# Strassen's scheme for 19 of 22 input slabs of one feed-forward, and a first slab on un-normed x in two others

## The chip, the cores and the metric

The program runs on one NeuronCore of a Trainium2 chip, in one launch. Its time is the device time of that core in microseconds. All engines of the core (TensorE, VectorE, ScalarE, GpSimd, SyncE) are programmed by hand, each with its own instruction stream, and meet through semaphores.

## The reference

Two small decoder blocks stand one after the other on x of 512 tokens by 1024 channels, everything in float32. The first block has two layers with adaptive norm (a hybrid mixer, then a retention mixer), the second has two layers (a MoBA and differential-attention mixer, then a dilated and latent-attention mixer). Each layer ends in a feed-forward of width 2816. The four feed-forwards are what the change is about:

```python
def swiglu(h, w_in, w_out):                      # first block: s0, s1
    g, u = split(h @ w_in)                       # 1024 x 5632
    return (silu(g) * u) @ w_out                 # 2816 x 1024

def conv_ffn(h, w_in, conv_w, conv_b, w_out):    # second block: c0, c1
    u, g = split(h @ w_in)
    g = causal_depthwise_conv(g, conv_w, width=3) + conv_b
    return (gelu(g) * u) @ w_out
```

Their input h is an RMS norm of x over the channels (in the first block with a scale and a shift from the condition).

## The kernel before

x lies transposed in SBUF: channels on the partitions, in eight tiles of 128 x 512 tokens. Every weight matrix comes from HBM in slabs of 1 MB (128 x 2048 float32; 128 x 1408 for the output slabs of the feed-forwards) into three buffers `raw`. To keep float32 precision on TensorE's fast fp32r format, each operand is kept as a high part and a remainder: ScalarE copies `raw` to `whi` (L200, `act_slab`), VectorE subtracts `raw - whi` to `wlo` (L211, `dve_slab`), and each 128x128 block is multiplied three times (`mm3`): hi by hi, lo by hi, hi by lo. There are two buffers each of `whi` and `wlo`, so slab n+2 can be split once slab n is multiplied.

A feed-forward runs in two halves. In a half, eleven input slabs (u = 0 to 10, then 11 to 21) each give one 128 x 512 tile of the gate and one of the other factor: 8 blocks along the channels x 2 tiles x 3 = 48 matmuls of 512 columns, in PSUM banks 2(u mod 2) and the next. In s0 and s1, ScalarE takes the SiLU out of PSUM (L762), VectorE multiplies (L841, the signal `gated`), ScalarE makes the high part (L766) and GpSimd the remainder (L856) of the product. Then eight output slabs multiply these eleven tiles (33 matmuls of 512 columns each), and VectorE adds the result to x. Every engine takes its work in the order in which its program is written; a wait holds all that stands behind it on that engine.

The norm ahead of s0 and s1: the first slab (`pe_first_slab`) is multiplied with x times its gain, not yet divided by the root mean square. Between its third and fourth channel block TensorE sums the squares, ScalarE makes 1/rms (`act_between`, `act_rs`), VectorE (L412), ScalarE (L430, L433) and GpSimd (L440) then write the normed h over the un-normed one behind TensorE, and VectorE multiplies the first slab's two tiles by `rs` (L806). The other 21 slabs take the normed h.

In c0 and c1 all 22 slabs take the un-normed x times gain. The sum of squares stands behind the first slab, and the division by the rms is made in every unit: VectorE takes the gate out of PSUM times `rs` (L820), starts the convolution with one tensor-scalar (L824) and two scalar-tensor-tensor taps (L827, twice), ScalarE takes the GELU (L753), GpSimd multiplies it by `rs` (L853), and VectorE multiplies with the other tile out of PSUM (L841).

## Time and profile before

| | |
|---|---|
| median of three timed runs | 2903.44 us (2899.37 to 2905.34) |
| the profiled execution's own time | 2905.31 us |
| its span in the profile | 2903.5 us |
| mean granted TensorE clock | 0.987 of full speed |
| instructions | 31988 |
| share of the chain that ended last: PE, DVE, ACT, POOL | 88%, 5%, 4%, 1% |
| stretch of s1 (first input slab loaded to the last output slab loaded) | 1250.7 to 1615.7 us |
| stretch of c0, by the same loads | 1883.1 to 2247.2 us |
| DMA, mean over the span | 102 GB/s |

The profile is one execution. PE is TensorE's matmuls, PEld its weight loads, DVE VectorE, ACT ScalarE, POOL GpSimd, SP SyncE. Matmuls are pipelined, so that the records of consecutive ones overlap: what a matmul costs in a stream is the distance between two starts, not its own duration. The chain that ended last goes back from the last instruction to what released each one; "issue" in it is time without a visible cause.

### The profile page before, as it was taken

To read this page: it belongs to the slowest core of one execution; us is meant where nothing else is said; L and a number is where in the kernel's file an instruction comes from. 1 tells how busy PE (TensorE), PEld (TensorE's weight loads), DVE (VectorE), ACT (ScalarE), POOL (GpSimd) and SP (SyncE) were. 2 spreads that over 40 slices of the span, in tenths; PEclk is the share of its full clock that TensorE was granted. 3 is DMA by queue.
4 is the path that set the end of the run, shared out by engine and by line. 5 is a ranking of instruction groups with operands and counts; after the bars stand their busy time and mean duration, and the time that the engine had idled before them with its cause. 6 is when DMAs were issued, how large, how long until landed. Compare 5 with 4: busy or idle time off the path is not lost.

```text
span 2903.5 us, 31988 instructions
## 1 busy us (share of the span) xinstructions
PE 2788.8 (96%) x13306; PEld 2209.4 (76%) x13306; DVE 1409.0 (49%) x2062; ACT 961.3 (33%) x1264; POOL 532.7 (18%) x414
## 2 busy tenths in 40 slices
PE   7998989999999999999999999899999998999998
...
GB/s 241 124 94 85 56 8 145 174 171 227 137 103 98 91 78 85 76 87 103 170 116 75 115 88 74 51 99 78 107 102 79 110 62 62 73 97 75 113 84 69
DMA packets 51088, 296.28 MB, mean 102 GB/s; under 512 B 6617, under 2 KB 6745, under 8 KB 25088
## 3 DMA queue, kind: packets, MB, share of 16 engines
...
## 4 chain that ended last, share of the span: by engine, by line
PE 88%; DVE 5%; ACT 4%; issue 1%; POOL 1%; DMA 0%; SPq 0%; DVEq 0%
PE ps L218 88%; DVE wlo L211 1%; PE ps L1321 1%; ACT whi L200 1%; DMA F<-in_ada 0%; ACT F L1338 0%; DVE F L412 0%; DVE F L2264 0%; DVE hl L416 0%; DVE ada L460 0%; ACT L253 0%; ACT E L2837 0%; DVE F L827 0%; ACT E L2835 0%; ACT hh L430 0%
## 5 line engine op out<-in xcount | busy, mean ns | idle before, releaser
L218 PE MATMUL ps<-hh,whi 128*128 128x512 f32 x2088 | 830.4, 398 | 11.5 <-ACT F L2815 5.8
L218 PE MATMUL ps<-hl,whi 128*128 128x512 f32 x2088 | 816.0, 391 | 0.0
L218 PE MATMUL ps<-hh,wlo 128*128 128x512 f32 x2088 | 815.2, 390 | 0.0
L211 DVE TENSOR_TENSOR wlo<-raw,whi 128x2048 fp32r<-128x2048 f32 (+2 forms) x235 | 496.6, 2113 | 513.7 <-ACT whi L200 511.5
L218 PE MATMUL ps<-R,whi 128*128 128x512 f32 x2080 | 651.4, 392 | 8.0 <-DVE wlo L211 3.1
L200 ACT ACTIVATE whi<-raw 128x2048 fp32r<-128x2048 f32 (+2 forms) x235 | 409.7, 1743 | 748.1 <-PE ps L218 743.6
L218 PEld LDWEIGHTS ps<-hh,whi 128*128 128x128 f32 x2088 | 393.7, 189 | 102.7 <-issue 12.3
L218 PEld LDWEIGHTS ps<-R,whi 128*128 128x128 f32 x2080 | 391.1, 188 | 95.8 <-issue 6.9
L218 PEld LDWEIGHTS ps<-hl,whi 128*128 128x128 f32 x2088 | 393.3, 188 | 83.7
L218 PEld LDWEIGHTS ps<-hh,wlo 128*128 128x128 f32 x2088 | 393.8, 189 | 82.3 <-issue 3.3
L218 PE MATMUL ps<-R,wlo 128*128 128x512 f32 x1040 | 405.4, 390 | 0.0
L218 PEld LDWEIGHTS ps<-R,wlo 128*128 128x128 f32 x1040 | 195.7, 188 | 40.5 <-issue 0.7
L856 POOL TENSOR_TENSOR R<-F,R 128x512 fp32r<-128x512 f32 x88 | 113.8, 1293 | 592.9 <-ACT R L766 592.9
L218 PE MATMUL ps<-F 64*64 64x32 f32 (+11 forms) x1160 | 189.0, 338 | 18.9 <-DMA tmp<-F 2.6
L218 PEld LDWEIGHTS ps<-F 64*64 64x64 f32 (+4 forms) x1160 | 114.8, 164 | 89.8 <-issue 61.9
L853 POOL TENSOR_TENSOR F<-F,rs 128x512 f32<-128x512 f32 x44 | 56.8, 1290 | 453.9 <-ACT F L753 453.9
L295 POOL TENSOR_TENSOR sacc<-sacc,tmp 128x512 f32<-128x512 f32 x45 | 79.5, 1766 | 312.9 <-ACT tmp L283 311.3
L766 ACT ACTIVATE R<-F 128x512 fp32r<-128x512 f32 x88 | 55.8, 634 | 237.6 <-DVE F L841 232.2
L841 DVE TENSOR_TENSOR F<-ps,F 128x512 f32<-128x512 f32 x86 | 59.1, 688 | 117.8 <-POOL F L853 90.9
L218 PE MATMUL ps<-whi,hh 128*128 128x512 f32 (+1 forms) x288 | 106.4, 369 | 4.9 <-ACT raw L2233 2.7
L218 PE MATMUL ps<-whi,hl 128*128 128x512 f32 (+1 forms) x288 | 105.4, 366 | 0.0
L218 PE MATMUL ps<-wlo,hh 128*128 128x512 f32 (+1 forms) x288 | 105.3, 366 | 0.0
...
## 6 DMA issues: line engine op xcount, KB each, us to landing
...
```

Source lines behind the costliest of these rows:

```text
L200: e.activation(m.whi[n % 2][:, 0:size], m.raw[m.slot[n]][:, 0:size], ACT.Copy).then_inc(*s.up("whi", n))
L211: e.tensor_tensor(m.wlo[n % 2][:, 0:size], m.raw[m.slot[n]][:, 0:size], m.whi[n % 2][:, 0:size].bitcast(F32), SUB).then_inc(*s.up("wlo", n))
L218: return e.matmul(out, l, r, start=start, stop=stop, skip_group_check=True)
L295: e.tensor_tensor(m.sacc[:, :], m.sacc[:, :], m.tmp[(n + 1) % 2], ADD).then_inc(*s.up("sacc", st, n))
L766: e.activation(m.o(j)[0], m.f(T2 + T * (u % 2)), ACT.Copy).then_inc(*s.up("gated_hi", st, u))
L841: e.tensor_tensor(out, m.ps[b + 1][:, :], a, MUL).then_inc(*s.up("gated", st, u))
L853: e.tensor_tensor(a, a, m.rs[:, :], MUL).then_inc(*s.up("gate_rs", st, u))
L856: e.tensor_tensor(lo, m.f(T2 + T * (u % 2)), hi.bitcast(F32), SUB).then_inc(*s.up("gated_lo", st, u))
L1321: t = e.transpose(m.ps[5 + (c + 1) % 2][:, i * P:(i + 1) * P], g.p(m, c)[:, i * P:(i + 1) * P], m.k("ident"))
```

## The change

In s1, slabs u = 3 to 21 are multiplied by Strassen's scheme (in Winograd's form). The 1024 x 256 weights of a slab are four quarters (two halves of the channels by the two tiles), h is four quarters (the same halves of the channels by tokens 0 to 255 and 256 to 511). Seven products of a quarter or a sum of quarters (0 to 6 in the code) replace eight. A product is 4 channel blocks x 3 = 12 matmuls of 256 columns, a slab 84. What that adds:

- **Weights.** VectorE forms four sums of quarters (128 x 512 each, L366 to L374), and seven pieces of 512 columns instead of four are split into `whi` and `wlo` (ScalarE L321, VectorE L352; pieces 1 and 2, and 4 and 5, go together where they lie side by side). `whi` and `wlo` become rings of eight places, each freed by the product that read it: piece i of the next slab takes the place that product i-1 of this one frees.
- **h.** Four sums of quarters (128 x 1024 each; three on VectorE, L1065, L1071, L1073, one on GpSimd, L1078), their high parts (ScalarE L1050) and remainders (three on VectorE, L1056, one on GpSimd, L1084), once, during slabs 0 to 3. ScalarE also adds the shift to the four even h tiles (L611).
- **Results.** A product's sum that another result needs too is copied out of PSUM by ScalarE while TensorE adds on: after product 1 (`open_out`, L990, 512 columns), after product 3 (`five_out`, L996, 256 columns; product 5 waits for it), after product 4 (`two_out`, L1000, 256 columns; product 6 waits for it). VectorE adds the copies to PSUM: `gate_sum` (L1158), `up_sum` (L1176). SiLU and the product then work from SBUF (L1024, L1218).

In c0 and c1 the first slab is treated as in s0 and s1 and the other 21 take the normed h (`act_between`, `dve_norm`, `pool_norm`). The multiplication by `rs` in each unit goes: VectorE copies the gate out of PSUM (L1202), ScalarE makes the convolution's first tap (`tap`, an Identity with scale and bias, L1015), VectorE the other two (L1193), and GpSimd's L853 is gone. The input slabs of all four feed-forwards lie in another order of columns in HBM (tile outside, channel block inside), with the same sizes.

The core of the diff:

```diff
-        self.whi = [sb(f"whi{i}", 2048, F32R) for i in range(2)]
-        self.wlo = [sb(f"wlo{i}", 2048, F32R) for i in range(2)]
+        self.whi, self.wlo = sb("whi", 4096, F32R), sb("wlo", 4096, F32R)
...
+PIECE = 512
+QUAD = ("fs0in", "fs1in", "fc0in", "fc1in")
+SEVEN = ("fs1in",)
+PLAIN = 3
+def is_seven(name, j):
+    return name in SEVEN and j >= PLAIN and (name == "fs1in" or (j - PLAIN) % 3 < 2)
+def ring_of(plan):
+    ring, free, held, at = [], [], [None] * 8, 0
+    for n, (name, j, _) in enumerate(plan):
+        if is_seven(name, j):
+            places = [(at + i) % 8 for i in range(7)]
+            free.append([held[p] for p in places])
+            for i, p in enumerate(places):
+                held[p] = ("product", n, i)
+            at = (at + 7) % 8
+        else:
+            at = -(-at // 4) * 4 % 8
+            places = [at + i for i in range(4)]
+            free.append([max((held[p] for p in places if held[p]), key=lambda x: (x[1], x[2]), default=None)])
+            for p in places:
+                held[p] = ("tile", n, "all")
+            at = (at + 4) % 8
+        ring.append(places)
+    return ring, free
...
+def act_piece(e, s, m, n, first):
+    for group in pieces_at_once(m, n, first):
+        i, size = group[0], PIECE * len(group)
+        piece_wait(s, m, n, group)
+        e.activation(m.piece(n, i, size)[0], m.source(n, i, size), ACT.Copy).then_inc(*s.up("whi", n, group[-1]))
+        if len(group) == 2:
+            s.also("whi", n, i)
...
+    if is_seven(*m.plan[n][0:2]):
+        dve_sum(e, s, m, n, 3)
+        for i in (0, 1):
+            dve_piece(e, s, m, n, i)
+        for i in (6, 4, 5):
+            dve_sum(e, s, m, n, i)
+        dve_piece(e, s, m, n, 3)
+        return
...
+    if i == 3:
+        e.tensor_tensor(s1, q[2], q[3], ADD).then_inc(*s.up("weight_sum", n, 3))
+    elif i == 6:
+        e.tensor_tensor(q[2], q[0], q[2], SUB).then_inc(*s.up("weight_sum", n, 6))
+    elif i == 4:
+        s.wait_ge("weight_sum", n, 3)
+        e.tensor_tensor(s2, s1, q[0], SUB).then_inc(*s.up("weight_sum", n, 4))
+    else:
+        s.wait_ge("weight_sum", n, 4)
+        e.tensor_tensor(s4, q[1], s2, SUB).then_inc(*s.up("weight_sum", n, 5))
...
+    for n in range(0, 8, 2) if gain in TURNED and st in MODULATED else ():
+        a, b = norm_slot(m, gain, n), m.mod[:, MOD[gain] + n:MOD[gain] + n + 1]
+        s.wait_ge("h_lo", gain, n)
+        e.activation(a, a, ACT.Identity, bias=b).then_inc(*s.up("h_sum", gain, n))
...
+def pe_seven(e, s, m, st, u):
+    name, l, conv = FFN[st]
+    n = m.at[name + "in", u]
+    w, x, y, z = seven_regions(m, u)
+    for i, out in enumerate((w, x, y, z, x, z, x)):
+        s.wait_ge("wlo", n, i)
+        if i == 0:
+            if is_seven(name + "in", u - 2):
+                s.wait_ge("up_sum", st, u - 2)
+            else:
+                s.wait_ge("gate_g" if conv else "gate", st, u - 2)
+            s.wait_ge("t_lo", st, 2)
+        elif i == 2:
+            s.wait_ge("gate_sum" if is_seven(name + "in", u - 2) else "gated", st, u - 2)
+        elif i == 3:
+            s.wait_ge("t_lo", st, 0)
+        elif i == 4:
+            s.wait_ge("open_out", st, u)
+            s.wait_ge("t_lo", st, 1)
+        elif i == 5:
+            s.wait_ge("five_out", st, u)
+        elif i == 6:
+            s.wait_ge("two_out", st, u)
+            s.wait_ge("t_lo_pool", st, 3)
+        hi, lo = m.piece(n, i)
+        for k in range(4):
+            t = mm3(e, out, hi[:, k * P:(k + 1) * P], lo[:, k * P:(k + 1) * P], *m.moving(i, k), i < 4 and k == 0, k == 3)
+        t.then_inc(*s.up("product", n, i))
...
+def act_seven(e, s, m, st, u):
     name, l, conv = FFN[st]
-    n, j, b = m.at[name + "in", u], u % 11, 2 * (u % 2)
-    a = m.f(T1 + T * (u % 2))
+    n, j, b, v = m.at[name + "in", u], u % 11, 2 * (u % 2), m.f(V4, 1024)
+    w, x, y, z = seven_regions(m, u)
+    nxt, after_plain = is_seven(*m.plan[n + 1][0:2]), not is_seven(*m.plan[n - 1][0:2])
+    for i in (4, 6) if after_plain else ():
+        act_piece(e, s, m, n, i)
+    if u == PLAIN:
+        s.wait_ge("tile", n - 1, "all")
+        act_turned(e, s, m, st, 3)
+    if nxt:
+        act_piece(e, s, m, n + 1, 0)
+    if j:
+        act_open_unit(e, s, m, st, u - 1)
+    if nxt:
+        act_piece(e, s, m, n + 1, 1)
+    s.wait_ge("product", n, 1)
+    if j and is_seven(name + "in", u - 1):
+        s.wait_ge("gate_sum", st, u - 1)
+        s.wait_ge("up_sum", st, u - 1)
+    e.activation(v[:, 0:512], m.ps[b][:, :], ACT.Copy).then_inc(*s.up("open_out", st, u))
+    if j:
+        act_close_unit(e, s, m, st, u - 1)
+    if nxt:
+        act_piece(e, s, m, n + 1, 3)
+    s.wait_ge("product", n, 3)
+    e.activation(v[:, 768:1024], z, ACT.Copy).then_inc(*s.up("five_out", st, u))
+    if nxt:
+        act_piece(e, s, m, n + 1, 4)
+    s.wait_ge("product", n, 4)
+    e.activation(v[:, 512:768], x, ACT.Copy).then_inc(*s.up("two_out", st, u))
+    if nxt:
+        act_piece(e, s, m, n + 1, 6)
+    else:
+        act_slab(e, s, m, n + 1)
...
+    if conv:
+        s.wait_ge("gate_sum" if seven else "gate_g", st, u)
+        e.activation(c, g, ACT.Identity, scale=m.col(f"fcw{l}", 44 + u), bias=m.col(f"fcb{l}", u)).then_inc(*s.up("tap", st, u))
+        return
...
+def dve_turn_first(e, s, m, st):
+    gain = NORM_OF[BEFORE[st]]
+    for n in range(8):
+        s.wait_ge("h_sum" if gain in MOD else "h_hi", gain, n)
+        s.wait_ge("h_lo_pool" if n % 2 else "h_lo", gain, n)
+    e.tensor_tensor(m.Hq(0, 0), m.Hq(0, 1), m.Hq(0, 0), SUB).then_inc(*s.up("t_sum", st, 0))
+def dve_turn_rest(e, s, m, st):
+    s.wait_ge("t_sum_pool", st, 3)
+    s.wait_ge("t_sum", st, 0)
+    e.tensor_tensor(m.Hq(1, 1), m.Hq(1, 1), m.Hq(0, 0), SUB).then_inc(*s.up("t_sum", st, 1))
+    s.wait_ge("t_sum", st, 1)
+    e.tensor_tensor(m.Hq(1, 0), m.Hq(1, 0), m.Hq(1, 1), SUB).then_inc(*s.up("t_sum", st, 2))
+def pool_turn(e, s, m, st):
+    s.wait_ge("t_sum", st, 0)
+    e.tensor_tensor(m.Hq(0, 1), m.Hq(1, 1), m.Hq(0, 1), SUB).then_inc(*s.up("t_sum_pool", st, 3))
+def pool_turned(e, s, m, st):
+    s.wait_ge("t_hi", st, 3)
+    hi, lo = m.turned(3)
+    e.tensor_tensor(lo, m.Hq(*TURNED_FROM[3]), hi.bitcast(F32), SUB).then_inc(*s.up("t_lo_pool", st, 3))
...
+                if u == 1 and st in TURN:
+                    dve_turn_rest(e, s, m, st)
+                if u == PLAIN - 1 and st in TURN:
+                    for i in (2, 0, 1):
+                        dve_turned(e, s, m, st, i)
...
+def dve_seven(e, s, m, st, u):
+    name, l, conv = FFN[st]
+    n, j, b = m.at[name + "in", u], u % 11, 2 * (u % 2)
+    nxt, after_plain = is_seven(*m.plan[n + 1][0:2]), not is_seven(*m.plan[n - 1][0:2])
+    for i in (4, 6) if after_plain else ():
+        dve_piece(e, s, m, n, i)
+    if j and is_seven(name + "in", u - 1):
+        dve_up(e, s, m, st, u - 1)
+    elif j and conv:
+        dve_gate_copy(e, s, m, st, u - 1)
+    if nxt:
+        dve_sum(e, s, m, n + 1, 3)
+        dve_piece(e, s, m, n + 1, 0)
+    if j and conv:
+        dve_taps(e, s, m, st, u - 1)
+    if nxt:
+        dve_piece(e, s, m, n + 1, 1)
+    if j:
+        dve_gated(e, s, m, st, u - 1)
+    for i in (6, 4, 5) if nxt else ():
+        dve_sum(e, s, m, n + 1, i)
+    for i in (3, 4) if nxt else ():
+        dve_piece(e, s, m, n + 1, i)
+    s.wait_ge("product", n, 5)
+    s.wait_ge("two_out", st, u)
+    if conv and u >= 2:
+        s.wait_ge("conv", st, u - 2)
+    g = m.f((GS if conv else T1) + T * (u % 2))
+    e.tensor_tensor(g, m.ps[b + 1][:, :], m.f(V4 + 256), ADD).then_inc(*s.up("gate_sum", st, u))
+    if nxt:
+        dve_piece(e, s, m, n + 1, 6)
+    else:
+        dve_slab(e, s, m, n + 1)
...
-        e.tensor_tensor(g, m.ps[b][:, :], m.rs[:, :], MUL).then_inc(*s.up("gate_g", st, u))
-        s.wait_ge("gate_g", st, u)
-        if u >= 2:
-            s.wait_ge("gate", st, u - 2)
-        e.tensor_scalar(c, g, w[2], m.col(f"fcb{l}", u), MUL, ADD).then_inc(*s.up("conv_k", st, u, 0))
-        for k in (1, 2):
-            s.wait_ge("conv_k", st, u, k - 1)
-            t = e.scalar_tensor_tensor(out=c[:, k:], in0=g[:, 0:T - k], scalar=w[2 - k], in1=c[:, k:], op0=MUL, op1=ADD)
-            t.then_inc(*(s.up("conv_k", st, u, 1) if k == 1 else s.up("conv", st, u)))
...
+def dve_gate_copy(e, s, m, st, u):
+    n, b = m.at[FFN[st][0] + "in", u], 2 * (u % 2)
+    s.wait_ge("tile", n, 0)
+    if u >= 2:
+        s.wait_ge("conv", st, u - 2)
+    e.tensor_copy(m.f(GS + T * (u % 2)), m.ps[b][:, :]).then_inc(*s.up("gate_g", st, u))
...
-        if conv:
-            a = m.f(T1 + T * (u % 2))
-            s.wait_ge("gate", st, u)
-            e.tensor_tensor(a, a, m.rs[:, :], MUL).then_inc(*s.up("gate_rs", st, u))
...
+    act_between(e, s, m, "even", m.at["fc0in", 0])
```

**VectorE in s1, one unit before** (`wlo` is the remainder of the next slab, `F<-ps,F` the product with the SiLU):

```order
L211 TENSOR_TENSOR wlo0<-raw2,whi0 128x2048
L841 TENSOR_TENSOR F<-ps3,F 128x512
L211 TENSOR_TENSOR wlo1<-raw1,whi1 128x2048
L841 TENSOR_TENSOR F<-ps1,F 128x512
L211 TENSOR_TENSOR wlo0<-raw0,whi0 128x2048
```

**The same place now, slab u = 5** (`raw2` holds the next slab; `sacc`, `tmp` and the third quarter of `raw2` take the sums):

```order
L1176 TENSOR_TENSOR F<-ps0,F 128x512
L366 TENSOR_TENSOR sacc<-raw2 128x512
L352 TENSOR_TENSOR wlo<-raw2,whi 128x512
L352 TENSOR_TENSOR wlo<-raw2,whi 128x1024
L1218 TENSOR_TENSOR F<-F 128x512
L368 TENSOR_TENSOR raw2<-raw2 128x512
L371 TENSOR_TENSOR tmp<-sacc,raw2 128x512
L374 TENSOR_TENSOR tmp<-raw2,tmp 128x512
L352 TENSOR_TENSOR wlo<-sacc,whi 128x512
L352 TENSOR_TENSOR wlo<-tmp,whi 128x1024
L1158 TENSOR_TENSOR F<-ps3,F 128x512
L352 TENSOR_TENSOR wlo<-raw2,whi 128x512
```

Two instructions a slab have become twelve; three of the four sums stand between the product with the SiLU (L1218) and the last pieces of the next slab.

**ScalarE in s1, one unit before** (`R<-F` is the high part of the unit's result):

```order
L200 ACTIVATE whi1<-raw1 128x2048
L762 ACTIVATE F<-ps0 128x512
L766 ACTIVATE R<-F 128x512
L200 ACTIVATE whi0<-raw0 128x2048
L762 ACTIVATE F<-ps2 128x512
L766 ACTIVATE R<-F 128x512
```

**The same place now** (`F<-ps` are `open_out`, `five_out` and `two_out`):

```order
L1024 ACTIVATE F<-F 128x512
L321 ACTIVATE whi<-raw2 128x1024
L990 ACTIVATE F<-ps2 128x512
L1041 ACTIVATE R<-F 128x512
L321 ACTIVATE whi<-sacc 128x512
L996 ACTIVATE F<-ps3 128x256
L321 ACTIVATE whi<-tmp 128x1024
L1000 ACTIVATE F<-ps2 128x256
L321 ACTIVATE whi<-raw1 128x512
```

The copies that TensorE waits for (L996, L1000) stand behind high parts that themselves wait for VectorE.

**VectorE in a unit of c0 before:**

```order
L211 TENSOR_TENSOR wlo1<-raw1,whi1 128x2048
L820 TENSOR_TENSOR F<-ps0,rs 128x512
L824 TENSOR_SCALAR F<-F,cols 128x512
L827 SCALAR_TENSOR_TENSOR F<-F,cols 128x511
L827 SCALAR_TENSOR_TENSOR F<-F,cols 128x510
```

**and now:**

```order
L342 TENSOR_TENSOR wlo<-raw1,whi 128x2048
L1202 COPY F<-ps0 128x512
L1193 SCALAR_TENSOR_TENSOR F<-F,cols 128x511
L1193 SCALAR_TENSOR_TENSOR F<-F,cols 128x510
L1224 TENSOR_TENSOR F<-ps1,F 128x512
```

The tensor-scalar has gone from VectorE to ScalarE.

## Rows read from the trace of the kernel before

**Rows 1.** Page, part 1: each engine's busy time, share of the span, instructions.

```profile
PE 2788.8 (96%) x13306; PEld 2209.4 (76%) x13306; DVE 1409.0 (49%) x2062; ACT 961.3 (33%) x1264; POOL 532.7 (18%) x414
```

**Rows 2.** Chain that ended last, 1230 to 1720: start us, us, piece.

```profile
1242.45 445.33 PE ps L218 x1964
```

**Rows 3.** Timeline, VectorE, plain slabs of s1: start us, us, instruction, [idle, releaser].

```profile
1324.13 2.29 DVE L211 TENSOR_TENSOR wlo<-raw,whi 128x2048 fp32r<-128x2048 f32 x1 [7.97 <-ACT whi L200]
...
1335.01 2.29 DVE L211 TENSOR_TENSOR wlo<-raw,whi 128x2048 fp32r<-128x2048 f32 x1 [7.99 <-ACT whi L200]
```

**Rows 4.** Timeline, TensorE, 256-column fp32r matmuls of the first mixer (40 starts apart).

```profile
89.33 0.28 PE L218 MATMUL ps<-wlo,hh 128*128 128x256 f32 x1
...
94.11 0.28 PE L218 MATMUL ps<-whi,hl 128*128 128x256 f32 x1
```

**Rows 5.** Groups by line and shape, VectorE: busy us, mean ns of one, idle before.

```profile
L211 DVE TENSOR_TENSOR wlo<-raw,whi 128x1408 fp32r<-128x1408 f32 x64 | 104.0, 1625 | 73.2 <-ACT whi L200 73.2
```

**Rows 6.** Groups by line and shape, ScalarE.

```profile
L200 ACT ACTIVATE whi<-raw 128x1408 fp32r<-128x1408 f32 x64 | 88.3, 1380 | 274.7 <-PE ps L218 274.7
L766 ACT ACTIVATE R<-F 128x512 fp32r<-128x512 f32 x88 | 55.8, 634 | 237.6 <-DVE F L841 232.2 <-DVE F L833 5.4
...
L433 ACT ACTIVATE F<-F,mod 128x512 f32<-128x512 f32 x12 | 8.7, 724 | 0.4
...
L1338 ACT ACTIVATE F<-ps 128x256 f32<-128x256 f32 x16 | 6.1, 384 | 8.7 <-PE ps L1321 8.7
```

**Rows 7.** Groups by line and shape, GpSimd.

```profile
L856 POOL TENSOR_TENSOR R<-F,R 128x512 fp32r<-128x512 f32 x88 | 113.8, 1293 | 592.9 <-ACT R L766 592.9
...
L2951 POOL TENSOR_TENSOR Rf<-Rf,csil 128x1024 f32<-128x1024 f32 x24 | 50.9, 2123 | 74.9 <-DMA Rf<-in_ada0h 74.8
```

**Rows 8.** Timeline, VectorE and GpSimd where they overlap, 1243 to 1271.

```profile
1243.00 5.54 POOL L1212 TENSOR_TENSOR R<-F,R 128x512 fp32r<-128x512 f32 x4 [22.25 <-ACT R L1110]
...
1247.48 3.21 DVE L211 TENSOR_TENSOR wlo<-raw,whi 128x2048 fp32r<-128x2048 f32 x1 [0.17 <-ACT whi L200]
...
1267.12 2.99 POOL L295 TENSOR_TENSOR sacc<-sacc,tmp 128x512 f32<-128x512 f32 x2 [8.41 <-ACT tmp L283]
...
1267.69 2.97 DVE L303 SCALAR_TENSOR_TENSOR hl<-x,acol,hh 128x512 fp32r<-128x512 f32 x2 [2.39 <-ACT hh L287]
```

**Rows 9.** Timeline, VectorE and ScalarE, third and fourth slab of s1.

```profile
1305.90 1.27 DVE L806 TENSOR_TENSOR F<-ps,rs 128x512 f32<-128x512 f32 x2
1307.70 2.29 DVE L211 TENSOR_TENSOR wlo<-raw,whi 128x2048 fp32r<-128x2048 f32 x1 [0.52 <-ACT whi L200]
...
1322.08 1.92 ACT L200 ACTIVATE whi<-raw 128x2048 fp32r<-128x2048 f32 x1 [5.26 <-PE ps L218]
```

**Rows 10.** Busy time by window (third from the end: granted clock), and the wait before.

```profile
519.00:523.00 4.00, 2.37 (x8) 1.90 (x9) 3.93 (x6) 1.82 (x2) 1.11 (x1) 0.82 0.94 334
523.00:527.00 4.00, 4.00 (x15) 3.24 (x14) 3.82 (x7) 1.10 (x2) 0.17 (x1) 0.76 0.49 195
...
520.63 0.47 PE L218 MATMUL ps<-hh,whi 128*128 128x512 f32 x1 [1.69 <-DVE wlo L211]
```

**Rows 11.** Chain that ended last, end of the first half of c0.

```profile
2038.27 0.70 DVE F L820
...
2039.00 0.56 DVE F L824
...
2041.87 1.30 POOL F L853
...
2043.19 0.70 DVE F L841
```

**Rows 12.** Timeline, TensorE, start and end of a half of c0.

```profile
1940.71 0.47 PE L218 MATMUL ps<-hh,whi 128*128 128x512 f32 x1 [0.33 <-issue]
...
2045.97 0.50 PE L218 MATMUL ps<-R,whi 128*128 128x512 f32 x1 [0.26 <-POOL R L856]
...
2047.60 0.50 PE L218 MATMUL ps<-R,whi 128*128 128x512 f32 x1 [0.66 <-DVE wlo L211]
```

More of the change, by code:

```diff
@@ L56 @@
     "dve_conv": "gate_g conv_k first_gate first_up first_qk shift_col",
+    "act_seven": "open_out five_out two_out",
+    "dve_seven": "gate_sum up_sum",
+    "dve_weights": "weight_sum",
+    "act_turns": "t_hi",
+    "pool_turns": "t_sum_pool t_lo_pool",
+    "dve_turns": "t_sum t_lo",
 }.items() for name in names.split()}
@@ L130, in __init__ @@
         self.rs = sb("rs", T)
[L131 removed]
+        self.tmps = sb("tmp", 2 * T)
+        self.tmp = [self.tmps[:, i * T:(i + 1) * T] for i in range(2)]
         self.ada = [sb(f"ada{i}", 256)[:, :] for i in range(2)]
         self.FN = 11040 + 2 * P
+        with nc.sbuf_tensor("Fr", [P, 6144], F32R) as self.Fr:
+            pass
         self.F = sb("F", self.FN)
@@ new lines, in w_rows, with piece, quad @@
+    def w_rows(self, n):
+        name, j, size = self.plan[n]
+        at, kc = PIECE * self.ring[n][0], KC.get(name, 8)
+        cut = lambda a: a[:, at:at + size].rearrange("p (k n) -> p k n", k=kc)
+        return cut(self.whi), cut(self.wlo)
+    def piece(self, n, i, size=512):
+        at = PIECE * self.ring[n][i]
+        return self.whi[:, at:at + size], self.wlo[:, at:at + size]
+    def quad(self, n, i, size=512):
+        return self.raw[self.slot[n]][:, PIECE * i:PIECE * i + size]
@@ L184, in sp_slab @@
     name, j, size = m.plan[n]
-    i = m.slot[n]
-    if m.slot_before[n] is not None:
-        s.wait_ge("wlo", m.slot_before[n])
+    i, before = m.slot[n], m.slot_before[n]
+    if before is not None:
+        s.wait_ge("wlo", before, len(m.ring_free[before]) - 1)
     elif i == 2:
@@ L205, in dve_slab, with dve_piece, dve_sum @@
         return
-    size = m.plan[n][2]
-    s.wait_ge(f"raw{m.slot[n]}", n)
-    if n >= 2:
-        s.wait_ge("tile", n - 2, "all")
-    s.wait_ge("whi", n)
-    e.tensor_tensor(m.wlo[n % 2][:, 0:size], m.raw[m.slot[n]][:, 0:size], m.whi[n % 2][:, 0:size].bitcast(F32), SUB).then_inc(*s.up("wlo", n))
+    size, at = m.plan[n][2], PIECE * m.ring[n][0]
+    if is_seven(*m.plan[n][0:2]):
+        dve_sum(e, s, m, n, 3)
[5 more added lines that the diff above has]
+        return
+    s.wait_ge(f"raw{m.slot[n]}", n)
+    if m.ring_free[n][0]:
+        s.wait_ge(*m.ring_free[n][0])
+    s.wait_ge("whi", n, 0)
+    e.tensor_tensor(m.wlo[:, at:at + size], m.raw[m.slot[n]][:, 0:size], m.whi[:, at:at + size].bitcast(F32), SUB).then_inc(*s.up("wlo", n, 0))
+def dve_piece(e, s, m, n, first):
+    for group in pieces_at_once(m, n, first):
+        i, size = group[0], PIECE * len(group)
+        piece_wait(s, m, n, group)
+        s.wait_ge("whi", n, group[-1])
+        hi, lo = m.piece(n, i, size)
+        e.tensor_tensor(lo, m.source(n, i, size), hi.bitcast(F32), SUB).then_inc(*s.up("wlo", n, group[-1]))
+        if len(group) == 2:
+            s.also("wlo", n, i)
+def dve_sum(e, s, m, n, i):
+    q = [m.quad(n, k) for k in range(4)]
+    s1, s2, s4 = m.sacc[:, :], m.tmp[0], m.tmp[1]
+    s.wait_ge(f"raw{m.slot[n]}", n)
+    before = max((k for k in range(n) if is_seven(*m.plan[k][0:2])), default=None)
+    if before is not None and i != 6:
+        s.wait_ge("wlo", before, i)
+    if i == 3:
+        e.tensor_tensor(s1, q[2], q[3], ADD).then_inc(*s.up("weight_sum", n, 3))
[7 more added lines that the diff above has]
+        e.tensor_tensor(s4, q[1], s2, SUB).then_inc(*s.up("weight_sum", n, 5))
 def mm(e, out, l, r, start=True, stop=True):
@@ L3307, in layout @@
             base = (0, 2816) if t == "s" else (2816, 0)
-            o[f"f{t}{l}in"] = slabs(wi[l], [two(base[0] + P * j, base[1] + P * j) for j in range(22)], 256)
+            w = slabs(wi[l], [two(base[0] + P * j, base[1] + P * j) for j in range(22)], 256)
+            o[f"f{t}{l}in"] = np.ascontiguousarray(w.reshape(22, P, 8, 2, P).transpose(0, 1, 3, 2, 4)).reshape(22, P, 2048)
             for n in range(2):
```

324 lines of the change are left out of this document (224 added, 100 removed).

## The prediction

> **What bounds the kernel now.** I read the page's first part first. TensorE is busy for 96% of the span, VectorE for 49%, ScalarE for 33%, GpSimd for 18% [rows 1]: time can only be won from TensorE's work or its waits. The chain of waits then says how s1 runs: from 1242.45 to 1687.8 it is one piece, 1964 matmuls of 445.33 us, with no wait of TensorE at all [rows 2]. A 512-column matmul there costs 445.33/1964 = 0.227 us, and a plain slab of 48 costs 10.88 us, the distance between two remainders [rows 3]. The two rows also show VectorE idle for 8 us in each slab. So s1 has the largest saving open to it, and nothing but TensorE's own work to lose; every wait that the change brings in is new time.
>
> In c0 and c1 TensorE waits a little: 0.33 us ahead of the third slab, and at the end of each half 0.26 us for the last remainder on GpSimd and 0.66 us for the second output slab's `wlo` [rows 12]. c1 shows the same, so the four half ends and two starts hold some 4.3 us.
>
> **The saving in s1.** 256-column fp32r matmuls with a new weight block each ran at (94.11 - 89.33)/40 = 0.1195 us [rows 4]. A slab in seven products is 84 x 0.1195 = 10.04 us, 0.84 less than 10.88; 19 slabs save **16.0 us**, if TensorE never waits. A weight load alone is recorded with 0.17 us (2209.4/13306, [rows 1]) and is hidden behind the matmul in both streams, or neither 0.227 nor 0.1195 could be. The Trainium skill (TensorE: Matmul & The Clock Gate, Part 3, "What overlaps and what doesn't") says that weight loads overlap matmuls in flight only in another row group. By that rule the loads would come on top; it is the last rival below. The trace disagrees with it.
>
> **The waits of a steady slab.** I follow one slab with order and rows, from the moment t = 0 at which product 1 is complete. A product is 12 x 0.1195 = 1.43 us; product 5 could start at 4.14, product 6 at 5.58.
>
> - ScalarE may only now write pieces 1 and 2 of the next slab: 1024 columns, between 0.634 and 1.380 [rows 6], by their line 1.06. Done at 1.09.
> - VectorE has `wlo` 1-2 behind it. 512 columns take 0.69 (L841, [rows 11]), 1408 take 1.625 [rows 5], so 1024 take 1.22. With 0.1 for the hand-off it is done at 2.41. Two instructions of 512 columns together took 1.27 [rows 9]: they follow one another every 0.6, less than each lasts. The product with the SiLU ends at 3.01.
> - ScalarE: high part of the result to 3.67 (0.634, [rows 6]), piece 3 to 4.20, `five_out` (0.384 for 256 columns, [rows 6]) to 4.50. Product 5 starts at 4.54: **0.40 us of waiting**.
> - VectorE meanwhile forms sum 6 and sum 4, to 4.23. Sum 5 needs sum 4 and would end at 4.93. But GpSimd asks for its remainder (1.293, [rows 7]) at 3.76, just after the high part. Both engines can't read two SBUF operands at once here: `wlo` took 3.21 us instead of 2.29 while GpSimd's L1212 ran, and ended 2.15 after it [rows 8]. Nor does a VectorE stream keep GpSimd out: two of each, asked for together, took 2.99 and 2.97 us [rows 8], so they went by turns. GpSimd comes in at 4.2 and sum 5 ends near 5.9, 1.0 later.
> - ScalarE can write pieces 4-5 only after that: to 6.99. `two_out` stands behind it: 7.28. Product 6 starts at 7.33 instead of 4.54 + 1.43 = 5.97: **1.35 us**.
>
> The Trainium skill (SBUF — State Buffer, "Who interferes with whom") has the shared port as an exclusive lock for a whole instruction, which whoever issues first holds, also against a VectorE instruction with two SBUF inputs. By it the delay is up to the full 1.29 instead of 1.0, and twelve slabs cost 3.5 us more; the trace had 0.92 for a partial overlap.
>
> A full slab thus takes 10.04 + 1.75 = 11.8 us, 0.9 more than a plain one. Which slabs are full: those that load a next one in products and close a unit, u = 5 to 9 and 13 to 19, twelve; in two of them pieces 4 and 5 lie apart in the ring and go singly (0.45 less): 12 x 1.75 - 0.9 = **20.1 us**. In u = 12 and 20 pieces 1 and 2 lie apart and the chain starts a product earlier: 0.8 each, **1.6 us**. u = 11 closes no unit, u = 4 has the small bias matmuls between its products, u = 10 and 21 load no next one: nothing.
>
> **The start of s1.** Plain slab 2 started at 1322.05 (when it released ScalarE, [rows 9]) - 0.16 - 10.88 = 1311.0, and its `wlo` was there at 1310.0 [rows 9]: 1.0 us to spare. Now four more ScalarE copies (2.5 us) stand ahead of its high part, VectorE waits for them with the first sum of h, and GpSimd's sum of 1024 columns (2.12, [rows 7]) then shuts VectorE out: `wlo` at 1314.1. Wait **3.2**. From there VectorE has the first product (0.7), two sums of h with GpSimd's remainder between (2 x 1.2 + 1.0), slab 3's sums and pieces (4.9) and the second product (0.7): 1323.8. ScalarE makes the high parts of the product and of a quarter (0.65 + 1.06), VectorE the remainder (1.3): 1326.9, while slab 2 ends at 1325.1. Wait **1.8**. In u = 3 follow on VectorE two remainders of h and `wlo` 4-5 (3.4), GpSimd's remainder of 1024 columns (2.3 in its way), three instructions of 512 columns, `wlo` 1-2 of the next slab and the product (3.7), then 1.5 on ScalarE: `five_out` at 1337.8 instead of 1334.2, **3.5**, and `two_out` 1.35 behind that as in a steady slab. With them the start costs 9.9 us, the least certain term: between 4 and 13.
>
> **The ends of the halves.** Output slab 0 is split only behind `two_out` and `gate_sum`. In the first half its place is free early; `wlo` (1.625) follows `gate_sum` and is 1.1 late. In the second its place is freed by product 5: 1.38 + 1.63 later TensorE has waited 2.0. **3.1 us.**
>
> **c0 and c1.** The tail ran 5.62 us from L820 to the end of L841 [rows 11]. Out go L824 (0.56) and L853 (1.30); in comes the tap (0.724, [rows 6]); the copy from PSUM costs what L820 did (0.70). With hand-offs it is 1.05 shorter. That is more than 0.26 + 0.66; about 0.1 stays, since `wlo` comes 1.05 earlier against 0.9. 4 x 0.9 = 3.6 us. The 0.33 ahead of the third slab goes too, as TensorE now waits for `first_up` alone: 0.6 in both. The norm that now runs behind the first slab is that of s1, which costs TensorE nothing; its cover is the second slab's 10.88 us, of which 1.0 was left over there, and here ScalarE has four instructions less. If that cover fails, up to 1 us each. **-4.2 us.** Relief of VectorE and GpSimd within these units is worth nothing: their slabs run at TensorE's pace.
>
> **The clock.** After the 1.69 us wait at 518.9 the granted clock fell to 0.82 and 0.76 in two stretches of 4 us: (0.18 + 0.24) x 4 = 1.7 us of full speed [rows 10]. The two long waits at s1's start should each bring such a fall: **+3.4 us**, between none and the third rival's.
>
> **Sum:** -16.0 + 20.1 + 1.6 + 9.9 + 3.1 - 4.2 + 3.4 = +17.9. On the profiled execution's 2905.3 that is 2923.2; this execution stood 1.9 above the median of 2903.4, so the median should be 2921.
>
> **The rivals.**
> 1. *GpSimd comes in behind sum 5.* Thirteen slabs (with u = 3) save 1.0 each: +5, 2908. For it: the request comes only half a microsecond before sum 5. Against: the turns in [rows 8]. Chance 0.14.
> 2. *Faster: `two_out` keeps up.* The place is product 6's wait. If the chain from product 1 to `two_out` stays under 5.6 us instead of 7.3, nothing ends later than TensorE: no steady waits, and half of the start. -16.0 + 5 + 3.1 - 4.2 = -12: 2891. For it: VectorE was idle for 8 us of each slab. Against: 1.7 us would have to go, more than the lock. Chance 0.17.
> 3. *The clock falls in steady slabs.* 0.40 and 1.35 lie a product apart, as much idle as the 1.69 that a fall followed. At 1.7 each, up to 12: +20, 2941. Against: the shorter waits of [rows 12] stood alone and the c0 slabs after them kept pace. Chance 0.13, with a part of it most likely.
> 4. *The halves don't save: weight loads add to short matmuls.* 84 x (0.12 + 0.17) - 10.88 = 13 a slab, +250. Against: [rows 4]. Chance 0.01.
>
> The forecast has 0.55. A difference of 0.2% (5.8 us) is about what a measurement can tell from none. Faster by more: 0.17, rival 2. Within: half of rival 1 and the forecast's low edge (small start, no clock falls, 0.2 off each steady slab), 0.09. Slower: 0.74. The range takes in rival 1, the low edge and most of the clock's cases: 2901 to 2936; rival 2 and the far end of rival 3 stay out.
>
> **What would show it.** Right: in s1 TensorE waits for ScalarE's L996 by 0.4 and for L1000 by 1.35 in every slab, L374 takes near 1.7 us instead of 0.69, two `gate_sum` lie 11.8 apart; three waits of over 1.5 us lie between slabs 1 and 4; no tail waits above 0.2 in c0. Wrong: slabs of 10.1 to 10.9 us, L374 at 0.69, or a second slab in c0 that TensorE waits behind. If GpSimd's remainder is not in VectorE's way the steady term fails; if `wlo` of slab 2 is in time the start does.

## The result and the profile after

| | before | after |
|---|---|---|
| median (4 runs each) | 2904.39 us | 2930.02 us |
| range | 2899.37 to 2907.12 | 2928.74 to 2932.11 |
| profiled execution (span) | 2905.3 (2903.5) | 2928.74 (2926.6) |

The ratio is 1.0087, 95% interval 1.0074 to 1.0099. The change costs 25 us, 22 to 29 by the interval. The forecast was +17.9, 2921 in the median, with 2901 to 2936 as its range. Direction and mechanism hold. The median lies 9 us above the forecast one, and the change is 7.4 larger than forecast (25.3 against 17.9).

The page's first part, after; TensorE is busy for 3.6 us less than in [rows 1], in a span that is 23 us longer, and the three others took over or lost some work:

```profile
PE 2785.2 (95%) x13990; PEld 2235.0 (76%) x13990; DVE 1543.8 (53%) x2245; ACT 1070.1 (37%) x1470; POOL 500.1 (17%) x380
```

Where [rows 2] had one piece of 445 us, the chain that ended last now changes engines in every full product slab. The rows are start, duration, piece, with short pieces between them left out; the first group is the start of s1, the second one full slab, the third the two half ends:

```profile
1306.73 1.82 ACT whi L295
1308.65 4.24 DVE wlo L342
...
1313.02 13.75 PE ps L378 x48
...
1363.29 4.54 PE ps L378 x36
...
1367.91 1.07 ACT whi L321
...
1369.31 0.94 issue
1370.25 0.68 DVE F L1218
...
1372.17 1.66 DVE tmp L374
...
1373.90 1.06 ACT whi L321
1374.96 0.28 ACT F L1000
1375.24 0.14 issue
1375.38 4.54 PE ps L378 x36
...
1422.81 0.93 issue
...
1610.66 1.87 issue
```

TensorE works for 4.5 us and then the chain runs for 7.5 us through the pieces of the next slab, the product with the SiLU (L1218), sum 5 (L374), the high part of pieces 4 and 5 and `two_out`, part of it beside TensorE's other work. In TensorE's own timeline (start, duration, instruction, and in brackets the idle time before it and what ended it) the same slab has two waits:

```profile
1371.81 0.28 PE L378 MATMUL ps<-Fr,whi 128*128 128x256 f32 x1
1372.45 0.39 PE L378 MATMUL ps<-hh,whi 128*128 128x256 f32 x1 [0.35 <-ACT F L996]
1372.67 0.28 PE L378 MATMUL ps<-hh,wlo 128*128 128x256 f32 x1
...
1373.86 0.28 PE L378 MATMUL ps<-hl,whi 128*128 128x256 f32 x1
1375.38 0.36 PE L378 MATMUL ps<-hh,whi 128*128 128x256 f32 x1 [1.24 <-ACT F L1000]
1375.57 0.28 PE L378 MATMUL ps<-hh,wlo 128*128 128x256 f32 x1
```

And VectorE and GpSimd beside them:

```profile
1371.45 0.68 DVE L371 TENSOR_TENSOR tmp<-sacc,raw 128x512 f32<-128x512 f32 x1
1372.17 1.65 DVE L374 TENSOR_TENSOR tmp<-raw,tmp 128x512 f32<-128x512 f32 x1
```

```profile
1371.68 1.59 POOL L1252 TENSOR_TENSOR R<-F,R 128x512 fp32r<-128x512 f32 x1 [10.49 <-ACT R L1041]
```

GpSimd's remainder asks at 1371.68, while sum 4 (L371) runs, and ends at 1373.27; sum 5 ends 0.55 after it, having taken 1.65 instead of 0.68. The groups by line and shape give it for the whole program:

```profile
L374 DVE TENSOR_TENSOR tmp<-raw,tmp 128x512 f32<-128x512 f32 x19 | 28.3, 1492 | 0.8
L378 PE MATMUL ps<-hh,whi 128*128 128x256 f32 x304 | 88.4, 291 | 24.3 <-ACT F L1000 16.0 <-ACT F L996 7.1 <-DVE wlo L352 1.2
```

So the new time is in s1. I measure the stage from the first squares matmul in its own first slab to the first squares matmul of the mixer behind it, since all versions have both: 1290.19 to 1660.55 before, 1288.68 to 1683.34 after, 370.4 and 394.7 us: **+24.3**. The same distance is used for every run below.

### The profile page after: what moved, and what is told of

Read it like the earlier page. It is cut to its first block, busy times and chain, and to the rows that moved or that the text cites. A ratio compares the mean times of both kernels' runs of the same rounds, so it can differ in the third digit from the quotient of the medians.

```text
span 2926.6 us, 33915 instructions
## 1 busy us (share of the span) xinstructions
PE 2785.2 (95%) x13990; PEld 2235.0 (76%) x13990; DVE 1543.8 (53%) x2245; ACT 1070.1 (37%) x1470; POOL 500.1 (17%) x380
## 4 chain that ended last, share of the span: by engine, by line
PE 83%; DVE 8%; ACT 5%; issue 2%; DMA 1%; POOL 1%; SPq 0%; DVEq 0%; ACTq 0%
PE ps L378 82%; DVE wlo L342 1%; ACT whi L321 1%; DVE tmp L374 1%; PE ps L1717 1%; ACT whi L295 1%; DVE F L2660 0%; DVE hl L585 0%; DMA F<-in_ada 0%; DVE tmp L371 0%; DVE raw L368 0%; DVE F L1218 0%; ACT F L1734 0%; ACT hh L604 0%; DVE F L580 0%
## 5 line engine op out<-in xcount | busy, mean ns | idle before, releaser
L378 PE MATMUL ps<-hh,whi 128*128 128x512 f32 (+1 forms) x2088 | 801.4, 384 | 40.2 <-ACT F L1000 16.0
L378 PE MATMUL ps<-hl,whi 128*128 128x512 f32 (+1 forms) x2088 | 784.2, 376 | 0.0
L378 PE MATMUL ps<-hh,wlo 128*128 128x512 f32 (+1 forms) x2088 | 783.6, 375 | 0.0
L342 DVE TENSOR_TENSOR wlo<-raw,whi 128x2048 fp32r<-128x2048 f32 (+2 forms) x216 | 455.6, 2109 | 385.4 <-ACT whi L295 385.2
L295 ACT ACTIVATE whi<-raw 128x2048 fp32r<-128x2048 f32 (+2 forms) x216 | 373.3, 1728 | 673.3 <-PE ps L378 668.5
L859 DVE SCALAR_TENSOR_TENSOR x<-ps,mod,x 128x512 f32<-128x512 f32 x56 | 41.2, 751 | 120.1 <-PE ps L378 120.0
L857 DVE TENSOR_TENSOR x<-ps,x 128x512 f32<-128x512 f32 x48 | 33.0, 691 | 129.9 <-PE ps L378 129.9
```

The costliest lines, as they stand in the source:

```text
L295: e.activation(m.whi[:, at:at + size], m.raw[m.slot[n]][:, 0:size], ACT.Copy).then_inc(*s.up("whi", n, 0))
L342: e.tensor_tensor(m.wlo[:, at:at + size], m.raw[m.slot[n]][:, 0:size], m.whi[:, at:at + size].bitcast(F32), SUB).then_inc(*s.up("wlo", n, 0))
L378: return e.matmul(out, l, r, start=start, stop=stop, skip_group_check=True)
L857: e.tensor_tensor(x, ps, x, ADD).then_inc(*s.up("x", *event))
L859: e.scalar_tensor_tensor(out=x, in0=ps, scalar=m.mod[:, gate + n:gate + n + 1], in1=x, op0=MUL, op1=ADD).then_inc(*s.up("x", *event))
```

## Experiments

Every experiment starts from the changed kernel, or from the one named.

### The convolutional part alone

```diff
-TURNED = ("nf1", "fn0", "fn1")
+TURNED = ("fn0", "fn1")
-TURN = ("s1",)
+TURN = ()
-SEVEN = ("fs1in",)
+SEVEN = ()
```

(`pe_toeplitz` stands behind plain slab 4 again, and its place in `F` is the old one.)

> Only the second part of the change: s1 runs in plain slabs and plain norm places as before, the convolutional blocks as in the change. Theory: the half ends and starts of c0 and c1 carry this part, and nothing else hangs on it: 2900 us against 2904 of the kernel before, -4.2 by the terms on record (4 x 0.9 and 2 x 0.3); by the distance of equal matmuls in the traces of before and after it is 2.0 in c0 and 2.1 in c1, so -4.1. In the profile no wait of TensorE above 0.2 us at the end of a first half. Rival: what the two blocks win is given back by the mixer between them or by the clock, 2904 within 2 us.

Measured: ratio 0.9986 (0.9975 to 0.9997), that is -4.1 us of 2906.4 (-7.3 to -0.9). s1 takes 370.4, as before. The tail waits at the end of a first half are gone; what is left of [rows 12] in c0 are these two, and c1 has the same:

```profile
1958.53 0.47 PE L378 MATMUL ps<-hh,whi 128*128 128x512 f32 x1 [0.40 <-issue]
...
2233.42 0.47 PE L378 MATMUL ps<-R,whi 128*128 128x512 f32 x1 [0.19 <-DVE wlo L342]
```

The size fits, one part of it doesn't. The 0.33 that [rows 12] had ahead of the third slab was to go. It went there, but 0.40 now stands ahead of the fourth: VectorE comes late to the taps of the second unit (1955.50 in its timeline), and that slab waits for the unit's gated product, which ends at 1958.42. I put the delay down to the eight norms before it; no run tests that. The half ends make up for it: from the first output matmul of the first half to that of the second, with the first half's end between, it is 181.02 before and 179.92 here in c0, 1.10 less where 0.9 was forecast. The part wins 4 us, and the loss is in s1. The interval doesn't quite shut out the rival, a win of at most 2 us; the waits that are gone from the trace speak against it.

### GpSimd's remainder behind sum 5

```diff
@@ pool_ffn
         s.wait_ge("gated_hi", st, u)
+        if u % 11 < 9 and is_seven(name + "in", u + 1) and is_seven(name + "in", u + 2):
+            s.wait_ge("weight_sum", n + 2, 5)
```

> The change, with one wait more: GpSimd's remainder of a result is asked for only when the fifth weight sum of the slab after next is formed. Theory (GpSimd and VectorE take turns at the two-operand reads, and GpSimd comes in ahead of sum 5): sum 5 takes 0.69 us instead of 1.65, TensorE's wait for two_out falls from 1.24 to about 0.3, the wait for five_out stays near 0.35; twelve slabs, u = 3, 12 and 20 win 0.9 to 1.0 each, 14 us: 2916. Rival (the chain over ScalarE, the SiLU and the high parts alone makes the wait, sum 5 is beside it): two_out waits go on near 1.2, 2929 within 2 us.

Measured: 1.0024 (1.0015 to 1.0033); s1 takes 381.0, 13.6 less than after the change. The two waits of a slab, the sum and the remainder now:

```profile
1371.90 0.39 PE L378 MATMUL ps<-hh,whi 128*128 128x256 f32 x1 [0.35 <-ACT F L996]
1373.88 0.36 PE L378 MATMUL ps<-hh,whi 128*128 128x256 f32 x1 [0.29 <-ACT F L1000]
```

```profile
1392.68 0.69 DVE L371 TENSOR_TENSOR tmp<-sacc,raw 128x512 f32<-128x512 f32 x1
1393.47 0.69 DVE L374 TENSOR_TENSOR tmp<-raw,tmp 128x512 f32<-128x512 f32 x1
```

```profile
1394.33 1.58 POOL L1254 TENSOR_TENSOR R<-F,R 128x512 fp32r<-128x512 f32 x1 [7.53 <-DVE tmp L374]
```

Sum 5 is back at 0.69, the wait for `two_out` at 0.29, and a full slab takes 11.13 instead of 12.08. The rival, by which sum 5 is beside the chain, falls. The 0.95 per slab is the share of the two engines' collision. The slab is still 1.13 above 10.00, since both waits stay, at 0.35 and 0.29.

### The same remainder made twice

```diff
@@ pool_ffn
+        if is_seven(name + "in", u):
+            e.tensor_tensor(lo, m.f(T2 + T * (u % 2)), hi.bitcast(F32), SUB).then_inc(*s.up("twice", st, u))
+            s.wait_ge("twice", st, u)
         e.tensor_tensor(lo, m.f(T2 + T * (u % 2)), hi.bitcast(F32), SUB).then_inc(*s.up("gated_lo", st, u))
```

> The change, with GpSimd's remainder of each product slab's result made twice in a row (same values). Theory (the engines take turns): the second instruction comes in behind sum 5, which still takes 1.65, and falls on VectorE's remainders that nothing waits for at once; TensorE's wait for two_out stays at 1.2 to 1.3, 2932 (the change's ratio of 1.0087) within 3 us. Rival (GpSimd, once in, keeps VectorE out until it is through): sum 5 takes 2.9, the wait becomes 2.5 in twelve slabs, +15 us, 2947.

Measured: 1.0076 (1.0062 to 1.0089), s1 394.6, full slabs 12.08: no more than with one.

```profile
1362.62 1.59 POOL L1253 TENSOR_TENSOR R<-F,R 128x512 fp32r<-128x512 f32 x1 [9.53 <-ACT R L1041]
1364.29 1.61 POOL L1255 TENSOR_TENSOR R<-F,R 128x512 fp32r<-128x512 f32 x1
```

```profile
1363.12 1.65 DVE L374 TENSOR_TENSOR tmp<-raw,tmp 128x512 f32<-128x512 f32 x1
1364.68 1.76 DVE L352 TENSOR_TENSOR wlo<-sacc,whi 128x512 fp32r<-128x512 f32 x1
```

The first instruction delays sum 5. The second starts 0.08 behind it in the records, while sum 5 is still on, yet sum 5 takes no longer than with one; the remainder behind sum 5 is what takes longer (1.76), and nobody waits for that. The rival, by which sum 5 takes 2.9, falls. The records fit engines that take turns, as [rows 8] suggested; the second GpSimd instruction does wait for a semaphore of the first, so that a gap between them isn't excluded as what let VectorE in.

### ScalarE's copies ahead of its other work

```diff
@@ act_seven
     e.activation(v[:, 0:512], m.ps[b][:, :], ACT.Copy).then_inc(*s.up("open_out", st, u))
+    s.wait_ge("product", n, 3)
+    e.activation(v[:, 768:1024], z, ACT.Copy).then_inc(*s.up("five_out", st, u))
     if j:
         act_close_unit(e, s, m, st, u - 1)
     if nxt:
         act_piece(e, s, m, n + 1, 3)
-    s.wait_ge("product", n, 3)
-    e.activation(v[:, 768:1024], z, ACT.Copy).then_inc(*s.up("five_out", st, u))
-    if nxt:
-        act_piece(e, s, m, n + 1, 4)
     s.wait_ge("product", n, 4)
     e.activation(v[:, 512:768], x, ACT.Copy).then_inc(*s.up("two_out", st, u))
+    if nxt:
+        act_piece(e, s, m, n + 1, 4)
```

> The change, with ScalarE's order in a product slab turned: five_out directly behind open_out, then the high part of the result and piece 3, then two_out, then pieces 4 and 5. GpSimd is left as in the change. Theory (TensorE waits only because the two copies stand behind work that waits for VectorE): no wait of TensorE in steady slabs although GpSimd still comes in between sums 4 and 5; a slab takes 10.04 us plus nothing, twelve slabs at 2.04, 3.5 us in u = 3 to 4, 12 and 20: 27 us less than the change, 2902. Rival 1 (the weight pieces then come late, since pieces 4 and 5 stand behind two_out): the waits move to products 3 and 4 of the next slab, over 1 us each, 2915 or more. Rival 2 (short matmuls carry a price of their own beside the waits): slabs without a wait still take over 10.4 us.

Measured: 0.9964 (0.9951 to 0.9976), 10 us under the kernel before and 36 under the change; s1 takes 365.2, 29.5 less than after the change, where 27 was expected. The remaining 6 of the 36 lie outside s1; the account behind the experiments comes back to them. The chain through s1 is TensorE's again:

```profile
1309.06 22.40 PE ps L378 x120
1331.47 1.30 issue
1332.77 73.38 PE ps L378 x604
1406.15 0.93 issue
1407.08 170.08 PE ps L378 x1188
1577.16 1.87 issue
```

VectorE's sum 5 still takes as long as after the change:

```profile
1393.72 1.67 DVE L374 TENSOR_TENSOR tmp<-raw,tmp 128x512 f32<-128x512 f32 x1
```

So the collision costs nothing once no copy stands behind it. Full slabs start 10.00 apart, 84 x 0.119: the products do save 0.88 a slab, rival 2 (a price of short matmuls) falls, and no wait came up at products 3 and 4, so rival 1 falls too. Left are the start and the two half ends.

### The start: its extra work without product slabs

The sums and copies stay, all slabs are plain, nothing reads the sums:

```diff
-SEVEN = ("fs1in",)
+SEVEN = ()
...
-                if u == PLAIN - 1 and st in TURN:
-                    for i in (2, 0, 1):
-                        act_turned(e, s, m, st, i)
```

(and the same for `dve_turned` and `pool_turned`; `pe_toeplitz` stands behind plain slab 4, as in the convolutional part alone)

> All slabs of s1 plain, the convolutional blocks as in the change, but the sums of the quarters of h and the four copies that they need stand where the change has them; nothing reads the sums. Theory (these copies alone make remainder of slab 2 late, and the clock fall belongs to the wait): a wait of 3.4 us before slab 2 and right behind it a stretch of 6.8 us at half clock, +6.8 against conv_only (2901.4): 2908. Rival (the fall belongs to the short matmuls of the product slabs that follow, or to chance): the wait alone, +3.4, 2905, granted clock 1.00 from 1308 to 1324.

Measured: 1.0001 (0.9992 to 1.0009), against 0.9986 of the convolutional part alone: +4.4 us between two ratios that are each known to 2 or 3 us. s1 itself is 376.8, +6.4. The wait, and the clock in the windows behind it (granted clock third from the end), beside those of the convolutional part alone:

```profile
1314.48 0.76 PE L378 MATMUL ps<-hh,whi 128*128 128x512 f32 x1 [3.45 <-DVE wlo L342]
```

```profile
1312.00:1316.00 4.00, 1.52 (x4) 1.26 (x5) 4.00 (x3) 1.00 (x3) 1.46 (x4) 0.67 0.27 57
1316.00:1320.00 4.00, 4.00 (x11) 3.13 (x10) 3.96 (x3) 1.94 (x2) 1.27 (x1) 0.50 0.54 227
```

```profile
1312.00:1316.00 4.00, 4.00 (x20) 3.30 (x19) 2.52 (x2) 2.94 (x4) 0.78 (x2) 1.00 0.32 78
```

The fall to the lower level (0.50 of full speed, 1.2 GHz) comes without a single product slab, so these have no part in it. It begins near 1313.3, while TensorE still waits. By the medians the rival's 3.4 can't be excluded; the trace of s1 decides for 6.4.

### The start: the extra work behind slab 2

From the version with the early copies of ScalarE:

```diff
@@ act_ffn
                 if u:
                     act_slab(e, s, m, n + 1)
+                if u == 1 and st in TURN:
+                    act_turn_in(e, s, m, BEFORE[st])
@@ dve_ffn
                 dve_slab(e, s, m, n + 1)
+                if u == 1 and st in TURN:
+                    dve_turn_first(e, s, m, st)
                 if j:
                     dve_ffn_unit(e, s, m, st, u - 1)
```

(`act_turn_in` holds the four copies that stood at the end of `act_norm`; `dve_turn_first` no longer stands in u = 0.)

> outs_first with the four copies and the first sum of h moved behind high part and remainder of slab 2, product slabs still from the fourth on. Theory (the work that must be done ahead of the first product slab is the bound, not its place in the queue): no wait before slab 2, 5 us of waiting before slab 3 instead of 3.4 before slab 2, the fall of 3.4 us behind that: within 2 us of outs_first, 2897. Rival (the wait was one of order): both go, 2890.

Measured: 0.9964 (0.9951 to 0.9977), no other than without it; s1 364.2 against 365.2.

```profile
1324.12 0.55 PE L378 MATMUL ps<-Fr,whi 128*128 128x256 f32 x1 [4.74 <-DVE Fr L1062]
```

The wait has moved to the first product slab, and a fall of the clock with it (0.57 between 1324 and 1328). It was not one of order, and the rival (2890) falls: VectorE can't have `wlo` of slab 2, four sums, three remainders of h and the first product pieces ready in two plain slabs.

### Start and half ends mended together, and the start alone

```diff
-PLAIN = 3
+PLAIN = 4
@@ ring_of
+        elif n and is_seven(*plan[n - 1][0:2]) and plan[n][2] <= 3 * PIECE and at <= 5:
+            places = [at + i for i in range(3)]
...
+            at = (at + 3) % 8
@@ act_seven
     e.activation(v[:, 0:512], m.ps[b][:, :], ACT.Copy).then_inc(*s.up("open_out", st, u))
+    if not nxt:
+        act_slab(e, s, m, n + 1)
@@ dve_seven
+    if not nxt:
+        dve_slab(e, s, m, n + 1)
     s.wait_ge("product", n, 5)
     s.wait_ge("two_out", st, u)
```

(with the two edits above; the second version leaves out everything but `PLAIN = 4` of this diff)

> outs_first with the start and the ends of s1 mended too: product slabs begin with the fifth slab, the four copies and the first sum of the quarters of h are made behind the high part and remainder of slab 2, and the first output slab of each half takes three places of the ring that are free after product 1 and is split ahead of two_out and gate_sum. Theory: no wait of TensorE over 0.3 us is left in s1, and so no fall of its clock there: 18 slabs save 0.84 each, -15.1, and the convolutional blocks -4.1: 19 us under the kernel before, 2885. Rival (the long waits at the start move behind the moved work, or the clock falls all the same): one or two waits of 2 us or more between slabs 1 and 5 and a fall of 3.4 us, 2892 to 2897.

> all4 without the mended half ends: product slabs from the fifth on, copies and sum behind slab 2, and the two copies of ScalarE early. Theory: a half end costs 1.9 here in both halves, since product 5 frees the place of the first output slab; 3.8 us more than all4, 2891.4, and no wait over 0.4 elsewhere in s1. Rival (the wait at the half end is hidden by the banks of the output slabs): 2888.

Measured: 0.9937 (0.9923 to 0.9950), 2887.6 us, for all of it, and 0.9958 (0.9945 to 0.9972) without the half ends. s1 takes 356.0 and 361.6. In the first version TensorE runs through the start of s1 without a wait (a piece of the chain), at full clock:

```profile
1236.75 90.42 PE ps L384 x394
```

```profile
1312.00:1316.00 4.00, 4.00 (x19) 3.30 (x19) 3.70 (x4) 0.63 (x1) 0.16 (x1) 1.00 0.13 16
```

In the second the half ends wait 1.87 each, and the clock falls behind the first of them:

```profile
1401.57 0.47 PE L378 MATMUL ps<-R,whi 128*128 128x512 f32 x1 [1.87 <-issue]
```

```profile
1400.00:1404.00 4.00, 2.43 (x9) 1.98 (x10) 2.76 (x3) 1.36 (x3) 0.39 (x1) 0.87 0.76 245
1404.00:1408.00 4.00, 4.00 (x14) 3.25 (x13) 1.63 (x1) 0.80 (x1) 0.89 (x1) 0.71 0.79 186
```

That is why the two are 5.6 apart in s1 and not 3.8. Both rivals fall: no long wait has moved behind the start, and the half ends are not hidden. The first version is 18.3 us faster than the kernel before (14.5 to 22.4), with 14.3 won in s1 and the 4.1 of the convolutional part. Eighteen slabs at 0.88 would be 15.8; the 1.5 between goes at least in part into short waits of TensorE, the longest of them 0.22 at 1357.46.

| s1, us | full slab | wait before slab 2 | half ends | s1 | ratio |
|---|---|---|---|---|---|
| before | 10.88 | 0 | 0 | 370.4 | 1 |
| the change | 12.08 | 3.44 and fall | 0.93, 1.87 | 394.7 | 1.0087 |
| remainder behind sum 5 | 11.13 | 3.44 and fall | 0.93, 1.87 | 381.0 | 1.0024 |
| early copies | 10.00 | 3.44 and fall | 0.93, 1.87 | 365.2 | 0.9964 |
| all mended | 10.00 | 0 | 0 | 356.0 | 0.9937 |

## Why the prediction was right, and where its size was off

In s1 the ledger is made from the distances of equal matmuls, slab by slab.

- **The saving.** Forecast 10.04 a slab and -16.0; it is 10.00 where nothing waits, 0.88 x 19 = -16.7. The rival of weight loads that add to short matmuls is out: 604 matmuls in 73.38 us are 0.1215 each, and a load alone is recorded with more, 0.189 in the mean for the 456 loads of products with `Fr` by `whi`. The Trainium skill (TensorE: Matmul & The Clock Gate, Part 3, "What overlaps and what doesn't") says that weight loads overlap matmuls in flight only where the row group differs, which would have put the loads on top; the trace contradicts it for these full blocks, and the measurement decides.
- **The steady slabs: right in mechanism, undersized.** Forecast 0.40 + 1.35 and 11.8; measured 12.08, 2.08 above 10.00, so 24.0 in twelve slabs instead of 20.1. That GpSimd gets in ahead of sum 5, at the moment forecast, is shown by the two runs on its remainder, and that the place of the copies on ScalarE makes a wait of it by the third. What failed is the term's size. The idle shown, 0.35 + 1.24, is even less than forecast; but from 1371.81 to 1372.45 are 0.64 where 0.12 is usual, and 0.10 more go in the next matmul's distance; the second wait costs 1.40 + 0.07 in that way. So of the 0.34 that a slab lacks in the forecast (2.09 by these starts, against 1.75), 0.17 are later starts of the two products (0.52 and 1.40 where 0.40 and 1.35 were forecast), and 0.17 the two slower first intervals, which the forecast had at nothing. The Trainium skill (Perfetto Trace Analysis, "Tensor Engine Instruction (MATMUL, LD_WEIGHTS)") says that the end of a matmul in the profile is computed, not observed. The trace agrees: records of 0.28 stand 0.12 apart. So I read TensorE's idle time from starts; the brackets are about 0.25 short of it.
- **Sum 5's delay.** Forecast 1.0, measured 1.65 - 0.68 = 0.97 in its record and 0.95 in the slab. The Trainium skill (SBUF — State Buffer, "Who interferes with whom") has the port that the two engines share as an exclusive lock; the trace agrees, since sum 5 ends only 0.55 after GpSimd. The delay of up to 1.29 that the forecast set beside this term is more than what came.
- **Slabs forecast at little or nothing.** u = 4 and u = 11 lose 0.5 and 0.6, forecast at nothing; u = 12 loses 0.9 and u = 20 1.0, forecast at 0.8 each. 1.4 us in all that the working left out, since it looked at these for whole waits and not for short ones.
- **The start: 2.6 too high, with one wait that didn't come.** Windows of the change (granted clock third from the end), and VectorE's timeline:

```profile
1308.00:1312.00 4.00, 1.59 (x7) 0.97 (x6) 3.64 (x2) 2.55 (x3) 3.37 (x3) 0.96 0.04 8
1312.00:1316.00 4.00, 2.98 (x7) 2.43 (x8) 3.96 (x4) 2.10 (x3) 1.53 (x1) 0.50 0.58 175
1316.00:1320.00 4.00, 4.00 (x13) 3.12 (x13) 4.00 (x6) 1.12 (x2) 0.00 (x0) 0.69 0.24 102
```

```profile
1324.03 1.47 DVE L1056 TENSOR_TENSOR Fr<-Rf,Fr 128x1024 fp32r<-128x1024 f32 x1 [1.65 <-ACT Fr L1050]
```

  The wait before slab 2 is 3.44 (forecast 3.2). The 1.8 before slab 3 didn't show: the first remainder of h is ready at 1325.5, and slab 2, slowed by the clock, ends only at 1326.59. At full clock it would have ended near 1323.9, and the wait would have come. The first product slab (u = 3) lost 4.4, forecast 4.9; its second wait (1.21) ended with the remainder of piece 6 (L352), not with `two_out`. Of the three waits of over 1.5 that the forecast named as its sign, two came, 3.44 and 2.68. The clock fell once, not twice, but for 3.4 us of full speed: (0.04 + 0.50 + 0.31) x 4, 0.7 of it while TensorE waited anyway. Start with clock: 3.6 + 2.7 + 4.4 = 10.7 against 9.9 + 3.4 = 13.3.
- **Half ends.** Forecast 1.1 and 2.0, measured 1.1 and 2.0 by distance (0.93 and 1.87 as idle).
- **c0 and c1.** -4.2 forecast, -4.1 measured with 3.2 to either side. That the sum fits so well is luck: the third slab's 0.33 was put off rather than saved, 0.6 of the term, and the half ends gave as much more.
- **The rivals.** GpSimd did not come in behind sum 5; where it was made to, the run gave 2912.4, near the 2908 of that rival. `two_out` keeps up only when it is moved: that run is 2897. No clock fall lies in the steady slabs.

The ledger gives +24.3 - 4.1 = +20.2; the profiled pair differs by 23.4, the median pair by 25. Against the forecast's 17.9, the steady slabs (3.9) and the short waits (1.4) were priced too low, the start (2.6) too high and the saving (0.7) too low: part of the undersized term was hidden by luck. The rest of the 25, some 5 us, lies in unchanged code. Up to s1 the profiled execution of the change was 1.5 us faster, and in the two later mixers 4.3 slower, where it spent 10 us more at the lower clock, which is 5 us of full speed. In ten profiled executions of the same code ahead of s1 the squares begin between 1284.5 and 1294.1 us, a scatter larger than this remainder. The seven other versions that hold the convolutional part beside work in s1 speak for scatter too: for each of them s1's difference less 4.1 comes within about 2 us of what its ratio gives, and the doubled remainder, with the same 394.6 in s1, is +22.1 by its ratio. Whether the change has a part in the rest stays open.
